# Prompt attention: the masks of a score unit together behind its wide matmuls, and the values of the preceding tile between the turned scores and the row scores

## The reference

```python
s_s = jnp.einsum('bqgrd,bqgksd->bqgrks', qr_b, kb) * scale
p_s = masked_softmax(s_s, m_s)
o_s = jnp.einsum('bqgrks,bqgksd->bqgrd', p_s, vb)
...
s_w = jnp.einsum('bqgrd,bkgd->bqgrk', qr_b, kw_b) * scale
p_w = masked_softmax(s_w, m_w)
o_w = jnp.einsum('bqgrk,bkgd->bqgrd', p_w, vw_b)
return g_b[..., 0:1] * o_c + g_b[..., 1:2] * o_s + g_b[..., 2:3] * o_w
```

## Time and profile before

| | |
|---|---|
| median of 3 runs | 1670.48 us (1670.05 to 1670.96) |
| span of the profiled execution, first to last instruction | 1663.0 us |
| PE busy in the span | 1605.1 us (97%), 13788 matmuls and as many weight loads |
| DVE, ACT, POOL busy | 824.2, 648.4, 117.2 us |
| prompt attention loop, `turned(0)` to the last `values` | 976.8 to 1146.6 us |

### The profile page before, as it was taken

One profiled execution on the slowest core, in us unless ns is written; L12 is line 12 of the kernel. 1 busy time (PEld: TensorE's weight loads), 2 busy tenths in 40 slices (PEclk: granted clock), 3 DMA queues, 4 the chain that ended last, 5 costly groups with the idle time before them and its releaser, 6 DMA issues.

```text
span 1663.0 us, 32232 instructions
## 1 busy us (share of the span) xinstructions
PE 1605.1 (97%) x13788; PEld 1472.4 (89%) x13788; DVE 824.2 (50%) x1091; ACT 648.4 (39%) x1141; POOL 117.2 (7%) x146
## 2 busy tenths in 40 slices
PE   8999899999999999999999779999999999999998
PEld 7787699999999999999999545556999999999998
DVE  6988547434343346633343465652473433434372
ACT  5444655323131334521232366665442222323242
POOL 1000000000000000010240352210000000000000
PEclk9999999999999999999999989999999999999999
DMA  7633161332323222322146200002223232322221
GB/s 204 160 93 113 35 206 56 104 98 77 102 77 100 78 82 71 102 83 77 53 135 211 92 1 1 1 14 77 76 77 102 76 102 77 102 77 87 92 77 54
DMA packets 139623, 145.69 MB, mean 88 GB/s; under 512 B 6562, under 2 KB 131314, under 8 KB 139279
## 3 DMA queue, kind: packets, MB, share of 16 engines
q1 hardware_dynamic: 138207, 136.94, 26.2%
q0 software_dynamic: 1280, 6.75, 1.3%
HBM read 130.79 MB, written 10.87 MB: 85 GB/s over the span
## 4 chain that ended last, share of the span: by engine, by line
PE 86%; DVE 7%; ACT 4%; issue 2%; DMA 0%; SPq 0%; DVEq 0%; ACTq 0%
PE ps L389 62%; PE ps L522 2%; PE ps L1215 2%; PE ps L1064 2%; PE ps L1063 2%; PE ps L1065 2%; PE ps L1737 2%; PE ps L1717 2%; DVE w_lo L374 1%; PE ps L1719 1%; PE ps L1664 1%; PE ps L575 1%; ACT w_hi L369 1%; PE ps L1662 1%; DVE resid L688 1%
## 5 line engine op out<-in xcount | busy, mean ns | idle before, releaser
L389 PE MATMUL ps<-x_hi,w_hi 128*128 128x272 f32 x1664 | 360.8, 290 | 11.5 <-DVE x_lo L2530 4.3
L389 PE MATMUL ps<-x_hi,w_lo 128*128 128x272 f32 x1664 | 357.8, 289 | 0.0
L389 PE MATMUL ps<-x_lo,w_hi 128*128 128x272 f32 x1664 | 356.6, 288 | 0.0
L374 DVE TENSOR_TENSOR w_lo<-w_raw,w_hi 128x2048 fp32r<-128x2048 f32 x101 | 233.8, 2315 | 141.4 <-ACT w_hi L369 139.5
L369 ACT ACTIVATE w_hi<-w_raw 128x2048 fp32r<-128x2048 f32 x101 | 192.6, 1907 | 267.6 <-PE ps L389 264.9
L389 PEld LDWEIGHTS ps<-x_hi,w_hi 128*128 128x128 f32 x1664 | 266.9, 189 | 20.5 <-issue 11.5
L389 PE MATMUL ps<-hid_hi,w_hi 128*128 128x272 f32 x1280 | 268.0, 289 | 2.2 <-DVE hid_lo L2038 1.5
L389 PE MATMUL ps<-hid_hi,w_lo 128*128 128x272 f32 x1280 | 267.4, 288 | 0.0
L389 PEld LDWEIGHTS ps<-x_lo,w_hi 128*128 128x128 f32 x1664 | 267.1, 189 | 0.0
L389 PE MATMUL ps<-hid_lo,w_hi 128*128 128x272 f32 x1280 | 266.6, 288 | 0.0
L389 PEld LDWEIGHTS ps<-x_hi,w_lo 128*128 128x128 f32 x1664 | 265.4, 189 | 0.0
(11 more groups left out here) (378 smaller groups left out, 2140.9 us busy)
## 6 DMA issues: line engine op xcount, KB each, us to landing
w_raw<-in_ffn_w_in SPq DMA_DIRECT2D x64, 512.0 KB, 4.5
w_raw<-in_ffn_w_out SPq DMA_DIRECT2D x64, 512.0 KB, 4.3
w_raw<-in_nsa_w_in SPq DMA_DIRECT2D x20, 512.0 KB, 4.5
w_raw<-in_ple_w_gate SPq DMA_DIRECT2D x16, 512.0 KB, 4.3
w_raw<-in_conv_w_in SPq DMA_DIRECT2D x15, 512.0 KB, 5.4
w_raw<-in_conv_w_out SPq DMA_DIRECT2D x8, 512.0 KB, 4.0
w_raw<-in_nsa_w_o SPq DMA_DIRECT2D x8, 512.0 KB, 4.5
conv_in_turned<-conv_in SPq DMA_DIRECT2D x16, 203.2 KB, 2.9
```

The costliest lines, as they stand in the source:

```text
L374: dve.tensor_tensor(WL[par][:, :], RAW[par][:, :], WH[par][:, :].bitcast(F32), ALU.subtract)\
L389: m = pe.matmul(o_, w[par][:, wcols:wcols + P], x[:, k, c_], start=f, stop=l)
```

## The change

In each score unit the two mask matmuls are taken out of the halves and issued together behind the four wide products. And `values(p - 1)` stands directly behind `turned(p)`, ahead of `scores(p + 8)`, where it stood at the end of the step. Nothing is added or removed; ACT, DVE and POOL run the same programs.

```diff
@@ scores(i)
+                masks = []
                 for x in range(2):
...
                     pe.matmul(out, qa[:, half, q], ka[:, br, 0:n], start=True, stop=False)
-                    pe.matmul(out[:, qt * P:n] if u < 2 else out[:, :, qt * P:n], IDB[:, :], mask, start=False, stop=False)
-                    m = pe.matmul(out, qb[:, half, q], kb[:, br, 0:n], start=False, stop=True)
+                    pe.matmul(out, qb[:, half, q], kb[:, br, 0:n], start=False, stop=False)
+                    masks.append((out[:, qt * P:n] if u < 2 else out[:, :, qt * P:n], mask))
+                for out, mask in masks:
+                    m = pe.matmul(out, IDB[:, :], mask, start=False, stop=True)
                 m.then_inc(S["s_full"], 1)
@@ turned(i)
                     pe.matmul(out, ka[:, br, k], qa[:, who, kt * P:SEQ], start=first, stop=False)
-                    pe.matmul(out[:, 0:P] if t < 4 else out[:, :, 0:P], CAUB[:, :], mask, start=False, stop=False)
-                    m = pe.matmul(out, kb[:, br, k], qb[:, who, kt * P:SEQ], start=False, stop=last)
+                    pe.matmul(out, kb[:, br, k], qb[:, who, kt * P:SEQ], start=False, stop=False)
+                    masks.append((out[:, 0:P] if t < 4 else out[:, :, 0:P], mask))
+                for x, (out, mask) in enumerate(masks):
+                    m = pe.matmul(out, CAUB[:, :], mask, start=False, stop=t < 5 or x == 1)
                 m.then_inc(S["t_full"], 1)
@@ steps()
                     turned(p)
+                    if p:
+                        values(p - 1)
                     if p + LEAD < N_S:
                         scores(p + LEAD)
...
                             cmp_scores(CMP_AT[p], p)
-                        values(p - 1)
                 values(N_T - 1)
```

More of the change, by code:

```diff
@@ L1715, in turned @@
                         br, who, mask, first = x, slice(0, 2), idb, t == 4 or x == 0
-                    last = t < 5 or x == 1
                     pe.matmul(out, ka[:, br, k], qa[:, who, kt * P:SEQ], start=first, stop=False)
-                    pe.matmul(out[:, 0:P] if t < 4 else out[:, :, 0:P], CAUB[:, :], mask, start=False, stop=False)
-                    m = pe.matmul(out, kb[:, br, k], qb[:, who, kt * P:SEQ], start=False, stop=last)
+                    pe.matmul(out, kb[:, br, k], qb[:, who, kt * P:SEQ], start=False, stop=False)
+                    masks.append((out[:, 0:P] if t < 4 else out[:, :, 0:P], mask))
+                for x, (out, mask) in enumerate(masks):
+                    m = pe.matmul(out, CAUB[:, :], mask, start=False, stop=t < 5 or x == 1)
                 m.then_inc(S["t_full"], 1)
```

## The result

The changed kernel takes 1683.97 us (median of 6 runs, 1676.74 to 1685.94) against 1670.26 us before (6 runs, 1663.45 to 1670.96): a ratio of 1.0091 with a 95% interval of 1.0071 to 1.0111. The forecast was 1684.2.

What follows compares the result with a forecast made beforehand. PE was taken to bound most loop steps, with a ring of PE, DVE and ACT queues only a little behind. A 7.4 + B 5.4 + C 4.9 - masks 4.0 = 13.7 us gave 1684.2 us, range 1677 to 1692.

Steps and rivals of the forecast that it cites:

- A: First turned scores of a pair: moved values no longer cover PE's wait for `q_row`; 7 by 1.05, 7.4 us slower.
- B: Second turned scores of a pair: values wait for DVE's bank copy, delaying row scores; 6 by 0.9, 5.4 us slower.
- C: Turned scores wait for exponentials standing behind later sums in ACT's queue; 4.9 us slower, bounds 3.1 and 8.
- The masks: Score units: grouping leaves fewer weight loads behind short 128-column masks; 4.0 us gain, bounds 0 and 6.3.
- one ring: Loop queues: row scores on PE, maxima on DVE, sums then exponential on ACT, back to PE; only a little behind PE.
- slab split: ACT's split of a weight slab, for which `turned(8)` already waited 0.79 us; some 0.6 us more.
- The clock: Rival: PE's pauses in the loop lower the granted clock over two steps of each pair; 10 us, 1694; chance 5%.
- the 7.5 us around the span: Whole launch: time outside the profiled span, taken as unchanged, from span 1676.7 to median 1684.2 us.
- covered after all: Rival: PE bounds, the holes at the two waits close and only the masks count; 1664.2 us; chance 4%.
- the pause at A: Rival: this pause lets ACT and DVE catch up, so B and C vanish; 1671.6 us, no change; chance 5%.

Runs made afterwards that it cites:

- masks_only: Changed kernel with the values put back at the end of the step, masks still grouped; loop 165.2 us, median 1664.4 us, ratio 0.9974 to before.
- a_rows: Changed kernel with shifts right behind the turned scores and DVE's `q_row` row ahead of the maxima, in steps 6c+5 alone; loop 179.0 us, median 1672.2 us.
- out_first: Changed kernel with DVE copying the bank of the values out ahead of the maxima; loop 184.2 us, median 1682.6 us, ratio 1.0096 to before.
- values_only: Kernel before with only the values moved, masks left inside the halves; loop 188.8 us, median 1688.3 us, ratio 1.0133 to before.
- split_moved: Changed kernel with ACT's split of the weight slab in step 11, not step 6; loop 184.1 us, median 1677.6 us, ratio 1.0071 to before.
- a_back: Changed kernel with the values back at the end of the step in steps 6c+5 alone; loop 181.6 us, median 1676.7 us, ratio 1.0059 to before.
- covered: Changed kernel with shifts right behind the turned scores, DVE's `q_row` row and bank copy ahead of the maxima, in all steps; loop 185.9 us, median 1682.5 us.

## Why the prediction was right

The direction, the places and the size came out. By step of the pair, the loop of the changed kernel differs from that of masks_only, and so by the move of the values alone, as follows (sums over the eight pairs, from the starts of the turned scores; steps 6c and 6c+1 are taken together, since a start behind the compressed product is recorded early):

| steps | us | predicted as |
|---|---|---|
| 6c+5 | +8.2 | A, 7.4 |
| 6c and 6c+1 | +5.2 | B, 5.4, and 0.6 of C |
| 6c+2 | +2.6 | C, 0.8 |
| 6c+3 | -0.1 | no wait |
| 6c+4 | +4.5 | C, 3.5 |
| all | +20.4 | 17.7 |

masks_only itself is 4.6 below before, so that 15.8 are left, against 13.7 predicted for the span.

- **The masks** were put at 4.0 with bounds 0 and 6.3. They gave 4.6 alone and, without step 8 and its lower clock, 4.5 with the moved values. (Of the 40 units of row scores 26 have masks of 128 columns, not 27; the full gain was 6.1.) That a weight load behind a mask of 128 columns is not hidden, as the earlier trace rows said, agrees with the load of 0.20 us that starts with the mask, and with the gain of masks_only. No run changes the load alone, so this cause is argued, not shown. The Trainium skill's page "TensorE: Matmul & The Clock Gate" (section "Part 2: What happens when you issue a matmul") says that weight loads are pulled ahead of matmuls in flight. The trace agrees: the load starts with the mask, ahead of its own product. That it is thereby hidden does not fit these rows.
- **A** is right in place and nearly in size: 8.2 by steps (1.20 to 1.22 in six places for 1.05, 0.94 in the last), 7.4 in the six steps of a_rows that the clock left alone.
- **B** is right in place; its wait was sized at 0.9, and PE's idle shows 0.66, six times. By steps, the third to the seventh pair grew by 0.62 to 0.85 us here, and B is 4.3 in all, 5.2 less the 0.9 in step 7 that belong to C. But its worth is not its wait: out_first took it away and got 1.4 us. I had treated B and C as a sum with a correction for one step. They are one ring; the pause at B gave the exponentials the slack that they lack without it.
- **C** was too small. By steps it is 7.8 (0.87 in step 7, then 2.6, 4.5 and -0.1), not 4.9. The tile-4 steps were 0.90 to 0.98 for 0.77 where there was no slack, and 0.28 to 0.31 for 0.22 where there was. The rest is the second pair: its slab split, sized at 0.6, cost 0.9 in step 7 and, with the lower clock, 1.5 in step 8.
- **The clock**, a rival with 5%, came true at this one place, for about 1.3 us, not twice a pair.
- The agreement of the median to 0.2 us is partly luck. In the loop the forecast was low by 2.1 us, since C was 2.9 too small and A 0.8, while B was 1.1 too large and the masks gave 0.6 more. And the 7.5 us around the span were about 1.8. With a spread of 10 us between executions, 15.8 us in the loop and 13.7 in the medians say the same.

The other two rivals fell. Nothing was covered after all, and the pause at A did not pay for B and C: they were there with it, and when a_rows took A away, the waits for exponentials grew by 0.6 us and those for the bank shrank by 0.6.

Values between the units cost PE nothing by themselves where this can be read. In the steps 6c+3, where the values have moved too but the traces list no wait of PE, the changed kernel and masks_only differ by 0.05 us at most; only with the masks left in the halves are these steps 0.1 us longer (values_only against before, from the second pair on). What stays open is why the loop starts up to 9 us apart in different executions.

## What to carry to other kernels

Before moving independent work of the bounding engine, ask what round trip it covers where it stands: here a microsecond of values hid a row on its way through DVE, and moved a few instructions ahead it hid nothing and delayed everything in strict queues behind. A wait's length is not what its removal is worth, when the next wait of the same ring stands close behind; take waits away one at a time and look at which one grows. And two edits that come together can have opposite signs: the masks alone are the better kernel.

## What the runs showed of the hardware that was not expected

Behind a pause of PE of about 2 us inside a busy loop the clock may fall, and need not. The same pause at the same place, 2.06 us ahead of `turned(41)`, left the clock up in the changed kernel (timeline, PE):

```profile
1147.53 0.39 PE L1720 MATMUL ps<-q_pair,k_hi_twice 128*128 128x256 f32 x1 [2.06 <-ACT pT L1817]
...
1148.11 0.39 PE L1724 MATMUL ps<-ident_bf,causal_bf 128*128 128x256 bf16 x2
```

and was followed by the lower level in split_moved:

```profile
1141.89 0.39 PE L1720 MATMUL ps<-q_pair,k_hi_twice 128*128 128x256 f32 x1 [2.06 <-ACT pT L1817]
...
1142.60 0.65 PE L1724 MATMUL ps<-ident_bf,causal_bf 128*128 128x256 bf16 x2
```

The two masks take 0.65 instead of 0.39 us. In a_back, behind 2.05 us, the granted clock is 0.56 over the next 3.9 us. Over all traces, the five pauses of 2.05 or 2.06 us at `turned(41)` were followed by the lower level in three kernels (a_rows too) and not in two (values_only too). At `turned(8)`, pauses of 1.77 to 2.51 us were followed by it in all five kernels that have them (granted clock 0.65 to 0.68 over the next 5 us), and one of 1.64 us in values_only was not. The pauses of 1.33 us at the start of a pair were followed by no such stretch in the changed kernel: from 1026 us to the end of its loop the granted clock is 1.00. But in covered it is 0.57 over the 4 us behind a pause of 1.36 us in step 11:

```profile
1023.63 0.70 PE L1698 MATMUL ps<-consts,shift_hi_lo 128*4 128x128 f32 x4 [1.36 <-DVE shift_hi_lo L1891]
```

So the length of a single pause does not tell in these traces whether the clock falls.
